# Gated projections and hidden layers: 512-column matmuls over both halves of the activations, summed by VectorE

## The reference

```
def squared_relu_mlp(x, w_up, w_down):          # D_FF = 4096
    return jnp.square(jax.nn.relu(x @ w_up)) @ w_down

def swiglu_ffn(x, w_in, w_down):                # D_FF_2 = 2816
    h = x @ w_in
    g, u = h[..., :D_FF_2], h[..., D_FF_2:]
    return (jax.nn.silu(g) * u) @ w_down

# GLA: q, k (512 wide each), v, r (1024 each) and a low-rank gate of x @ w_in
# HGRN: q = silu(proj[:, :1024]), f = proj[:, 1024:2048], v, gate;
#       k = (1 - lb) * sigmoid(-f), decay = lb + (1 - lb) * sigmoid(f)
```

## Time and profile before

| | us |
|---|---|
| median of 3 runs | 1345.78 |
| lowest, highest | 1345.62, 1347.33 |
| the profiled execution, its time | 1347.31 |
| the profiled execution, its span | 1345.2 |
| TensorE matmul busy | 1295.3 |
| TensorE weight load busy | 1173.2 |
| VectorE busy | 798.5 |
| ScalarE busy | 604.5 |
| mean granted clock of TensorE | 0.985 |

### The profile page before, as it was taken

How to read it: one execution, slowest core, us unless ns; L and a number is a source line. 1 busy time by engine, 2 the same in 40 slices (tenths; PEclk the granted TensorE clock), 3 DMA queues, 4 the chain that set the end, 5 groups by cost and what they waited for, 6 DMA issues and landing times.

```text
span 1345.2 us, 19149 instructions
## 1 busy us (share of the span) xinstructions
PE 1295.3 (96%) x8247; PEld 1173.2 (87%) x8247; DVE 798.5 (59%) x929; ACT 604.5 (45%) x738; POOL 95.4 (7%) x222
## 2 busy tenths in 40 slices
PE   7888999999998999999999999999999989999998
PEld 6777899998887899998888999998898879999996
DVE  5775755556655755556775544456766657444464
ACT  5464544444723444444553434445532236443334
POOL 4240100001000200000321000000000001000000
PEclk9899999999998999999899999999999989999999
DMA  8320655555642555554534555554643317555542
GB/s 291 114 75 19 234 188 187 188 188 166 195 145 75 198 179 190 187 189 143 171 116 162 191 188 188 188 188 157 214 147 113 128 49 237 184 183 184 186 156 93
DMA packets 130836, 221.06 MB, mean 164 GB/s; under 512 B 6936, under 2 KB 99120, under 8 KB 130752
## 3 DMA queue, kind: packets, MB, share of 16 engines
q1 hardware_dynamic: 127728, 209.83, 46.4%
q0 software_dynamic: 3024, 10.01, 2.4%
HBM read 218.77 MB, written 1.05 MB: 163 GB/s over the span
## 4 chain that ended last, share of the span: by engine, by line
PE 87%; DVE 5%; ACT 4%; DMA 2%; POOL 1%; issue 1%; ACTq 0%; DVEq 0%; POOLq 0%
PE ps L541 19%; PE ps L542 19%; PE ps L543 19%; PE ps L564 19%; PE ps L845 3%; PE ps L652 2%; DVE wlo L1615 2%; PE ps L708 2%; ACT whi L1195 1%; DMA raw<-in_mlp_w_up 1%; DMA raw<-in_ffn_w_in 1%; PE ps L950 1%; ACT rot L1225 1%; ACT xh L1212 1%; PE ps L814 1%
## 5 line engine op out<-in xcount | busy, mean ns | idle before, releaser
L1615 DVE TENSOR_TENSOR wlo<-raw,whi 128x2048 fp32r<-128x2048 f32 (+3 forms) x203 | 453.8, 2243 | 231.9 <-ACT whi L1195 231.4
L1195 ACT ACTIVATE whi<-raw 128x2048 fp32r<-128x2048 f32 (+3 forms) x203 | 378.2, 1869 | 161.6 <-DMA raw<-in_mlp_w_down 40.9
L541 PE MATMUL ps<-xh,whi 128*128 128x256 f32 x1240 | 351.9, 284 | 0.0
L543 PE MATMUL ps<-xl,whi 128*128 128x256 f32 x1240 | 351.6, 284 | 0.0
L542 PE MATMUL ps<-xh,wlo 128*128 128x256 f32 x1240 | 351.5, 283 | 0.0
L541 PEld LDWEIGHTS ps<-xh,whi 128*128 128x128 f32 x1240 | 238.7, 192 | 2.0 <-issue 0.3
L542 PEld LDWEIGHTS ps<-xh,wlo 128*128 128x128 f32 x1240 | 238.6, 192 | 1.6
L543 PEld LDWEIGHTS ps<-xl,whi 128*128 128x128 f32 x1240 | 238.6, 192 | 0.0
L541 PE MATMUL ps<-whi,hh 128*128 128x512 f32 x432 | 169.0, 391 | 0.0
L542 PE MATMUL ps<-whi,hl 128*128 128x512 f32 x432 | 168.6, 390 | 0.0
L543 PE MATMUL ps<-wlo,hh 128*128 128x512 f32 x432 | 168.1, 389 | 0.0
(11 more groups left out here) (337 smaller groups left out, 1258.8 us busy)
## 6 DMA issues: line engine op xcount, KB each, us to landing
raw<-in_ffn_w_in SPq DMA_DIRECT2D x44, 1024.0 KB, 5.1
raw<-in_mlp_w_up SPq DMA_DIRECT2D x32, 1024.0 KB, 5.4
raw<-in_mlp_w_down SPq DMA_DIRECT2D x32, 1024.0 KB, 4.9
raw<-in_ffn_w_down SPq DMA_DIRECT2D x22, 1024.0 KB, 4.9
raw<-in_hgrn_w_in SPq DMA_DIRECT2D x16, 1024.0 KB, 5.3
raw<-in_b_w_in SPq DMA_DIRECT2D x12, 1024.0 KB, 5.3
raw<-in_ple_w_gate SPq DMA_DIRECT2D x8, 1024.0 KB, 6.5
raw<-in_a_w_in SPq DMA_DIRECT2D x6, 1024.0 KB, 5.3
```

The source lines that it names most:

```text
L541: mm(o, a[0], b[0], start=start, stop=False)
L543: return mm(o, a[0], b[1], start=False, stop=stop)
L1195: a.activation(whi[:, slot, 0:w], raw[:, slot, 0:w], ACT.Copy).then_inc(s["hi_done"], 1)
L1615: v.tensor_tensor(wlo[:, slot, 0:w], raw[:, slot, 0:w], whi[:, slot, 0:w].bitcast(F32), ALU.subtract).then_inc(s["lo_done"], 1)
```

## The change

- `xh` and `xl` become two halves of one tensor `xhl`, so that the 256 tokens of a block's high part and of its remainder lie side by side as 512 columns.
- `side_by_side(n, b)` takes the place of `columns` for 77 chunks: for each block, 8 matmuls of `whi` with both halves (512 columns, one whole bank), then 8 of `wlo` with the high half into the first 256 columns. A chunk fills two banks, and the value is the sum of the two halves of each bank.
- VectorE makes that sum (`sum_parts`, a `tensor_reduce` from two banks into SBUF) for each such chunk. The readers, ScalarE mostly, take it from SBUF. In the MLP VectorE also takes the relu and the square in one pass, and ScalarE only copies the high part.
- MLP: the loop is hidden(g + 2), then down(g); the chunk order follows. Groups alternate between banks 6, 7 and 4, 5. FFN: gates go to banks 6, 7, ups to 4, 5.
- New waits of TensorE: `up_summed`, `gate_summed`, `side_summed` before a bank pair is written again; in GLA `keys_summed` 2 before the first value chunk; in HGRN `half_summed` before most chunks and before the first value chunk.
- In HGRN VectorE's program gets the sums between remainders, gates and decay steps; the sums of f1.0 and f1.1 stand ahead of the first decay step's pick.

```
@@ tensors and chunk order
-        xh = sb("xh", [P, KD, SEQ], F32R)
-        xl = sb("xl", [P, KD, SEQ], F32R)
+        xhl = sb("xhl", [P, KD, 2, SEQ], F32R)
+        xh, xl = xhl[:, :, 0, :], xhl[:, :, 1, :]
...
-                if 1 <= q <= MLP_GROUPS - HOLD:
-                    chunk(f"down{layer}.{q - 1}", rows_of(down, 2 * q - 2, 2, 0, D), 2, D)
+                if 2 <= q <= MLP_GROUPS - HOLD + 1:
+                    chunk(f"down{layer}.{q - 2}", rows_of(down, 2 * q - 4, 2, 0, D), 2, D)
@@ TensorE
+            def side_by_side(n, b):
+
+                take(n)
+                w = weights(n, KD, FG)
+                for f in range(2):
+                    for kk in range(KD):
+                        mm(bank(b + f), w[0][:, kk, P * f : P * f + P], xhl[:, kk, :, :].rearrange("p a n -> p (a n)"), start=(kk == 0), stop=False)
+                    for kk in range(KD):
+                        last = mm(bank(b + f, 256), w[1][:, kk, P * f : P * f + P], xh[:, kk, :], start=False, stop=(kk == KD - 1))
+                last.then_inc(s["w_done"], 1)
...  MLP
                 def hidden(g):
-                    take(up(g))
-                    columns(weights(up(g), KD, FG), bank(4 + g % 3)).then_inc(s["w_done"], 1)
+                    if g == 3:
+                        pe.wait_ge(s["h_act"], 2 * layer + 2)
+                    if g >= 4:
+                        pe.wait_ge(s["up_summed"], sums(layer, g - 2))
+                    side_by_side(up(g), 6 - 2 * (g % 2))
 
                 for g in range(MLP_GROUPS - HOLD):
-                    if g > 0:
-                        hidden(g + 1)
+                    hidden(g + 2)
                     pe.wait_ge(s["h_lo"], hcount(layer, 0, g) + 1)
                     take(dn(g))
                     down(dn(g), g % 3, g == 0)
-                for g in range(MLP_GROUPS - HOLD + 1, MLP_GROUPS):
-                    hidden(g)
+                hidden(MLP_GROUPS - 1)
...  FFN
                 def hidden(g):
-                    for w, n in enumerate((gn_(g), un(g))):
-                        take(n)
-                        columns(weights(n, KD, FG), bank(4 + 2 * (g % 2) + w)).then_inc(s["w_done"], 1)
+                    if g >= 2:
+                        pe.wait_ge(s["gate_summed"], (FFN_GROUPS - 1) * layer + g - 1)
+                    side_by_side(gn_(g), 6)
+                    if g == 1:
+                        pe.wait_ge(s["h_prod"], FFN_GROUPS * layer + 1)
+                    else:
+                        pe.wait_ge(s["side_summed"], (FFN_GROUPS - 1) * layer + g - 1)
+                    side_by_side(un(g), 4)
...  GLA
             for q in range(2):
                 n = first["gla_k"] + q
-                take(n)
                 pe.wait_ge(s["qk_out"], q + 1)
-                columns(weights(n, KD, FG), bank(4 + q)).then_inc(s["w_done"], 1)
-
+                side_by_side(n, 2 * q)
+
+            pe.wait_ge(s["keys_summed"], 2)
...  HGRN
+            def half_columns(name, q, summed):
+                if summed:
+                    pe.wait_ge(s["half_summed"], summed)
+                side_by_side(first[name] + q, 2 * q)
+            half_columns("hgrn_f0", 1, 0)
+            pe.wait_ge(s["f_out"], 1)
+            half_columns("hgrn_q0", 0, 0)
+            half_columns("hgrn_q0", 1, 1)
             for q in range(2):
+                half_columns("hgrn_f1", q, 2 + q)
+            decay_steps(1, HGRN_EARLY[0])
             for q in range(2):
+                half_columns("hgrn_q1", q, 4 + q)
                 decay_steps(1, HGRN_EARLY[1 + q])
+            pe.wait_ge(s["half_summed"], 7)
@@ ScalarE, HGRN
+                    if (w, q) == (0, 0):
+                        act.wait_ge(s["w_done"], n + 1)
+                        forget = bank(0)
+                    else:
+                        act.wait_ge(s["half_summed"], 4 * w + q)
+                        forget = pair(g4[w])
+                    a.activation(pair(k4[w]), forget, ACT.Sigmoid, scale=-1.0).then_inc(s["k_sig"], 1)
+                    act.wait_ge(s["k_sig"], 2 * w + q + 1)
+                    a.activation(pair(g4[w]), forget, ACT.Sigmoid).then_inc(s["f_out"], 1)
...
+                    act.wait_ge(s["half_summed"], 4 * w + q + 2)
+                    a.activation(queries, queries, ACT.Silu).then_inc(s["qk_out"], 1)
@@ VectorE
+            def sum_parts(n, b, dst):
+
+                dve.wait_ge(s["w_done"], n + 1)
+                return v.tensor_reduce(dst.rearrange("p (f n) -> p f n", f=2), ps[:, b : b + 2, :].rearrange("p f (a n) -> p f n a", a=2), AX_X, ALU.add)
...  MLP, g >= 2
                         ahead(up(g))
+                        sum_parts(up(g), 6 - 2 * (g % 2), r).then_inc(s["up_summed"], 1)
+                        dve.wait_ge(s["up_summed"], sums(layer, g))
+                        v.scalar_tensor_tensor(full, r, 0.0, r, ALU.max, ALU.mult).then_inc(s["h_full"], 1)
...  FFN, g > 0
                         ahead(gn_(g))
+                        sum_parts(gn_(g), 6, sig).then_inc(s["gate_summed"], 1)
                         ahead(un(g))
+                        sum_parts(un(g), 4, prod).then_inc(s["side_summed"], 1)
...
+                        v.tensor_tensor(prod, prod, sig, ALU.mult).then_inc(s["h_prod"], 1)
...  GLA, after the tree
-            ahead(first["gla_k"] + 1)
+            for q in range(2):
+                ahead(first["gla_k"] + q)
+                sum_parts(first["gla_k"] + q, 2 * q, k4[0][...]).then_inc(s["keys_summed"], 1)
...  HGRN
+            ahead(first["hgrn_f0"])
+            summed_half("hgrn_f0", 1, g4[0])
+            summed_half("hgrn_q0", 0, q4[0])
             gates(0)
+            summed_half("hgrn_q0", 1, q4[0])
             dve.wait_ge(s["att_zeroed"], 2)
             decayed_queries(0)
             for q in range(2):
+                summed_half("hgrn_f1", q, g4[1])
             decay_steps(1, HGRN_EARLY[0])
+            summed_half("hgrn_q1", 0, q4[1])
             gates(1)
             decay_steps(1, HGRN_EARLY[1])
+            summed_half("hgrn_q1", 1, q4[1])
             decay_steps(1, HGRN_EARLY[2])
             decayed_queries(1)
```

More of the change, by code:

```diff
@@ L1260, in mlp @@
                         act.wait_ge(s["rows_turned"], 2 * ROWS_AT[j] + g + 1)
+                        a.activation(r, bank(4 + g), ACT.Relu).then_inc(s["h_act"], 1)
+                        act.wait_ge(s["h_act"], 2 * layer + g + 1)
+                        a.activation(hh[:, slot, :], r, ACT.Square).then_inc(s["h_hi"], 1)
                     else:
                         ahead(up(g))
[L1263 to L1266, removed]
+                        act.wait_ge(s["h_full"], MLP_GROUPS * layer + g + 1)
+                        a.activation(hh[:, slot, :], buf[2][:, 512 * slot : 512 * slot + 512], ACT.Copy).then_inc(s["h_hi"], 1)
                     if g == 0:
                         rows_copy(j, up(0) - 1, 1, 1)
-                    if 1 <= g <= MLP_GROUPS - HOLD:
+                    if 2 <= g <= MLP_GROUPS - HOLD + 1:
                         ahead(up(g) + 1)
@@ L1285, in ffn @@
                         ahead(gn_(g))
-                        act.wait_ge(s["w_done"], gn_(g) + 1)
-                    a.activation(sig, bank(4 + 2 * sl), ACT.Silu).then_inc(s["h_act"], 1)
+                        act.wait_ge(s["gate_summed"], (FFN_GROUPS - 1) * layer + g)
+                    a.activation(sig, bank(4) if g == 0 else sig, ACT.Silu).then_inc(s["h_act"], 1)
                     if g == 0:
@@ L1429, in projected @@
             def projected(q):
[L1430 to L1431 removed]
+                dst = q4[0][:, 2 * q : 2 * q + 2, :].rearrange("p h n -> p (h n)")
+                a.activation(dst, bank(4 + q), ACT.Copy, scale=float(P**-0.5)).then_inc(s["qk_out"], 1)
             act.wait_ge(s["rows_turned"], 2 * ROWS_AT[T_X2] + 1)
@@ L1736, in ffn @@
                         ahead(gn_(g))
+                        sum_parts(gn_(g), 6, sig).then_inc(s["gate_summed"], 1)
                         ahead(un(g))
+                        sum_parts(un(g), 4, prod).then_inc(s["side_summed"], 1)
+                        dve.wait_ge(s["side_summed"], (FFN_GROUPS - 1) * layer + g)
+                        dve.wait_ge(s["h_act"], acts(layer, g))
+                        v.tensor_tensor(prod, prod, sig, ALU.mult).then_inc(s["h_prod"], 1)
                     else:
@@ L1996, in _ @@
             v_logs.then_inc(s["gate_logs"], 1)
-            ahead(first["gla_k"] + 1)
+            for q in range(2):
+                ahead(first["gla_k"] + q)
+                sum_parts(first["gla_k"] + q, 2 * q, k4[0][:, 2 * q : 2 * q + 2, :].rearrange("p h n -> p (h n)")).then_inc(s["keys_summed"], 1)
             dve.wait_ge(s["masks_done"], 1)
             dve.wait_ge(s["att_zeroed"], 1)
-            dve.wait_ge(s["qk_out"], 4)
+            dve.wait_ge(s["qk_out"], 2)
             dve.wait_ge(s["gate_exps"], 1)
@@ L2139, in decayed_queries, with summed_half @@
             def decayed_queries(w):
-                dve.wait_ge(s["qk_out"], 6 + 2 * w)
```

(17 more changed lines are left out.)

40 lines of the change are left out of this document (8 added, 32 removed).

## The result

The changed kernel took 1353.22 us (median of 5, 1351.37 to 1355.38) against 1346.36 us (1345.62 to 1348.22) for the kernel before: ratio 1.0044, 95% interval 1.0031 to 1.0056. It is 0.44% slower, on the side that was forecast and inside the range, but further than forecast: +6.9 us by the medians and +5.9 by the ratio, where +3.2 was expected.

The account below looks back on a forecast made before the run. TensorE's matmul count times spacing bounds MLPs and FFNs; gated stages also wait on VectorE. A 13.1 us gain against 6.4, 2.3, 7.1 and 0.5 lost gave +3.2, so 1349.0 us, range 1344 to 1355.5.

Parts of the forecast that it names:

- The pace: MLPs and FFNs: 16 fixed parts of 13.3 ns go per chunk; 68 x 0.193 = 13.1 us gained.
- the small term of 0.02 us for the change of width: Column chunks: each adds about one return trip between 512 and 256 columns, 0.02 us, taken off the 0.21 us gain.
- Sums at 1.22 us, hidden in MLPs and FFNs: VectorE: each chunk's added tensor_reduce takes 1.22 us, and in MLPs and FFNs costs TensorE nothing.
- GLA: GLA stage: TensorE idles 7.7 us for the second key sum, 6.4 us lost, plus 2.3 us for the lower clock.
- HGRN: HGRN stage: TensorE idles 6.7 us before decay step 1, values start later; 7.1 us lost, bounds 5.5 and 8.5.
- the clock's term in HGRN: HGRN after the restart at decay step 1: half clock costs 2.0 us until q1.0 ends.
- short sums: Rival: sums priced by outputs, 0.68 us each, six on the chain, 3.2 us back, 1345.8 us; chance 0.14.
- long sums: Rival: sums of pairs read at a large stride take 2.3 us, giving 1357 us; chance 0.12.
- a gain that fails: Rival: the matmuls' fixed part doesn't go, 1364 us, or near 1362 by the skill's formula; chance 0.06.
- cheaper widths: Rival: changing matmul width costs less than read, 16.4 us and more gained, near 1342 us; chance 0.08.
- The rival in which the clock holds: TensorE's clock after the stops holds or falls for less: 4 us back, 1345 us; chance 0.14.
- The sum: Whole kernel: -13.1 + 6.4 + 2.3 + 7.1 = +2.7, plus 0.5 for handovers: net +3.2 us.

Follow-up runs that it names:

- E3: The changed kernel with each 512-column matmul issued as two of 256 columns into halves of the same bank: 1365.63 us, ratio 1.013 to the kernel before.
- E1: The changed kernel with the nine chunks of GLA and HGRN put back to the code before: 1336.06 us, ratio 0.9904 to the kernel before.
- E2: The changed kernel with only GLA's two key chunks put back: 1344.98 us, ratio 0.9983 to the kernel before.
- E4: The changed kernel with 56 unused matmuls filling GLA's stop before the wait for the key sums: 1351.12 us, ratio 1.0027 to the kernel before.
- E10: The changed kernel once more, unedited, as the last kernel of the study: 1355.05 us, ratio 1.0047 to the kernel before.
- E9: The changed kernel with 44 and 18 unused matmuls filling two stops of HGRN: 1348.19 us, ratio 1.0005 to the kernel before.
- E7: The changed kernel with the widths in turn within a block (512, 256, 512, 256): 1357.43 us, ratio 1.0069 to the kernel before.

## Why the prediction was right, and where its sizes were off

- **The pace** (forecast 0.193 us a chunk, 13.1 us for 68): E3 has 0.19 a chunk, E1 12.9 us. Right. It is the gain less the small term of 0.02 us for the change of width: without that E3 would have 0.21 (see the last section). The term is too small in the FFNs. Their loop had one return trip between widths per group of two chunks and has four now, so 1.5 are added per chunk and not one, which makes 20 x 0.183 = 3.7 us a stage instead of 3.9; 3.6 were measured. The formula of the Trainium skill, TensorE: Matmul & The Clock Gate, section Back-to-back issue gap, would have 3 us saved. E1 and E3 both speak against it here: 0.19 us for 16 removed matmuls is 12 ns for each, the cost of the width change already taken off.
- **Sums at 1.22 us, hidden in MLPs and FFNs**: right, 1.222 measured, windows without idle TensorE, E1.
- **GLA** (forecast 6.4 + 2.3 = 8.7 us): the second sum ended at 361.3, by the same four pieces of VectorE's queue; the stop was 7.2 us where 7.7 was forecast, the clock cost 2.0. E2 has 8.3 us for both together, E4 2.4 for the clock. Right, within what one trace can tell (E10's has a stop of 8.6 and 3.0 for the clock).
- **HGRN** (forecast 7.1, of it about 2 for the clock, and 0.5 for handovers in all): the order of events came as walked through. With the stage 1.5 us later in this execution, the values were forecast at 1020.5 and came at 1019.9. There two small errors cancel: the stop was 5.75 us and not 6.7, since the pick ended at 998.0 where 998.9 was forecast, and the clock cost 2.5 us up to there (1.6 on decay step 1, 0.9 on q1.0) and not 2.0. But E1 and E2 leave about 11 us for this stage. **The step that failed in size is the clock's term in HGRN.** I let it end with q1.0 and wrote of the values that "from there the pattern is that of before". The chain shows the lower clock again on the first value chunk (1.8 us above 5.54) and on the second (1.6), so 5.9 us in all, and E9 gives about 5.5 back. In E10's trace the same places cost 7.7. The two chunks follow stops of 2.45 and 1.6 us, which I had counted as harmless. The second stop was there before, without a slow value chunk behind it; why the clock fell there now, no run shows. E9 shows only that it stays up when the two stops ahead of it are filled.
- **The rivals**: short sums and long sums are ruled out by the 1.222 us, a gain that fails and cheaper widths by E3. The rival in which the clock holds had the right lever and the wrong sign: the clock fell for more, not for less.
- **The sum.** By the stretches, the four MLPs and FFNs gained 12.2 us (2.7, 2.6, 3.6 and 3.3), GLA lost 6.7 and HGRN 10.5, and MLA's clock 1.3, together +6.3. By the ratios, 12.9 us gained and 19 lost make +6, but this second sum closes of itself, since the 19 is the distance from E1 to the changed kernel. The forecast of +3.2 lacks about 3 us, and the 3.4 us on the two value chunks of HGRN are of that size.

## What to carry to other kernels

Where TensorE bounds a stage and VectorE has room, two 256-column matmuls with the same weights are worth merging into one of 512 with a later sum. In a stage whose chain passes through VectorE, the same sum costs what stands ahead of it in VectorE's queue, so walk that queue forward, and put each sum in front of work that nobody waits for yet. Price every stop twice: its own length and the slower clock that may stand behind it. Here that happened behind stops of 1.6 and 2.45 us too. A stop filled with matmuls whose results nobody reads shows how much of it is the clock. And before a row of a table by stage is put down to the change, compare the granted clock of that stretch in the executions: here it moved unedited stretches by 1 to 3 us.

## What the runs showed that was not expected

- A change of width has a price that grows within the run behind it. In the changed kernel's chain of waits, the first 512-column run of a chunk, behind the 512-column matmuls of `down`, takes 1.81 us for 8; the second, behind 256-column ones, 1.84:

```profile
179.60 1.81 PE ps L691 x8
181.41 0.95 PE ps L693 x8
182.36 1.84 PE ps L691 x8
```

  So a return trip costs some 0.02 to 0.03 us when runs of 8 alternate (the forecast's small term), but only 0.007 a pair when single matmuls do (E7). 16 pairs at 0.007 are 0.11 us a chunk, against some 0.05 for the two trips that a chunk has in the changed kernel (one more than before, which is what the forecast counts). Over 68 chunks that is about 4 us, and 3.2 were measured, which agrees within the noise. What in the engine makes the cost stays open.
- The lower clock also slows the 64-column matmuls of the decay steps: 3.65 us for 16, where they take 2.0 at full clock.
